# Heads of 64 dimensions issued in pairs on TensorE, and the operand tensors placed anew in memory

## What is computed

```
def dilated_attention(q, k, v, ...):          # 16 heads of 64, first attention
    s = einsum('...qd,...kd->...qk', q, k); p = softmax(mask(s)); o = p @ v
def ssd_chunked(x, dt, a, b_mat, c_mat):      # 16 heads of 64, state space
    l_mat = exp(where(causal, a_cs[t] - a_cs[s], -inf)); y = (c @ b^T * l_mat * dt) @ x
def dsa_attention(q, k, v, qi, ki, wi, topk): # 16 indexer heads of 64
    logits = einsum('bqhd,bsd->bqhs', qi, ki) * IDX_DIM ** -0.5
    score = einsum('bqh,bqhs->bqs', wi, relu(logits)); idx = top_k(score, topk)
```

## The kernel before, in words

| data | before | after |
|---|---|---|
| WH, WL ring slot 0, 1, 2, 3 | 96, 224, 352, 480 | 256, 256, 256, 256 |
| XH, XL | 160 | 320 |
| MH, ML, AH2, AL2, AH4, AL4 | 288 | 320 |
| XH minus WH, modulo 256, slot 0, 1, 2, 3 | 64, 192, 64, 192 | 64, 64, 64, 64 |
| AH2 minus WH, modulo 256, slot 0, 1, 2, 3 | 192, 64, 192, 64 | 64, 64, 64, 64 |

## Time and profile before

### The profile page before, as it was taken

The page is one execution under the profiler, slowest core; times in us unless marked ns, Lnnn a source line. Parts: engine busy times, 40 slices in busy tenths (PEclk is TensorE's granted clock), DMA queues, the critical chain, the costliest instruction groups (busy, mean ns, idle before and its releaser), DMA issues.

```text
span 2735.8 us, 52761 instructions
## 1 busy us (share of the span) xinstructions
PE 2678.4 (98%) x22440; PEld 2616.3 (96%) x22440; DVE 1788.1 (65%) x2601; ACT 1340.9 (49%) x1811; POOL 111.8 (4%) x75
## 2 busy tenths in 40 slices
PE   8999999999999999999999999999899999999996
PEld 8998889899999999999899999999899999999996
DVE  6787679675555555555677786556676656665666
ACT  5464566454344443444344684444365435543543
POOL 2000021010000000000000000000400000000003
PEclk9999999999999999999999999999899999999998
DMA  6534445455555555555454456555355555555552
GB/s 236 180 136 142 155 139 173 151 193 193 193 193 193 193 193 195 193 193 188 143 171 139 164 176 202 194 196 178 134 190 195 193 194 193 194 193 193 194 191 85
DMA packets 136603, 488.45 MB, mean 179 GB/s; under 512 B 15152, under 2 KB 17584, under 8 KB 136368
## 3 DMA queue, kind: packets, MB, share of 16 engines
q1 hardware_dynamic: 136368, 485.09, 52.2%
HBM read 482.93 MB, written 2.10 MB: 177 GB/s over the span
## 4 chain that ended last, share of the span: by engine, by line
PE 94%; DVE 4%; ACT 1%; issue 1%; DMA 0%; SPq 0%; ACTq 0%; DVEq 0%
PE ps L753 93%; PE ps L756 1%; DVE WL L1694 1%; DVE xT L1694 1%; DVE XL L1702 1%; DVE T L1694 1%; DMA cst<-in_cst 0%; ACT xT L1177 0%; ACT WH L1177 0%; DVE small L1702 0%; DVE q L1694 0%; ACT P L1177 0%; DVE small L1694 0%; DVE AL L1702 0%; DVE P L1698 0%
## 5 line engine op out<-in xcount | busy, mean ns | idle before, releaser
L1694 DVE TENSOR_TENSOR WL<-raw,WH 128x1024 fp32r<-128x1024 f32 x907 | 1122.6, 1240 | 775.6 <-ACT WH L1177 774.9
L1177 ACT ACTIVATE WH<-raw 128x1024 fp32r<-128x1024 f32 x907 | 961.1, 1060 | 1317.5 <-PE ps L753 1316.0
L753 PE MATMUL ps<-XH,WH 128*128 128x256 f32 x5024 | 1406.9, 280 | 25.0 <-issue 10.8
L753 PE MATMUL ps<-XL,WH 128*128 128x256 f32 x5024 | 1393.0, 277 | 0.0
L753 PE MATMUL ps<-XH,WL 128*128 128x256 f32 x5024 | 1392.7, 277 | 0.0
L753 PEld LDWEIGHTS ps<-XH,WH 128*128 128x128 f32 x5024 | 945.0, 188 | 33.3 <-issue 28.2
L753 PEld LDWEIGHTS ps<-XL,WH 128*128 128x128 f32 x5024 | 944.6, 188 | 2.3 <-issue 1.5
L753 PEld LDWEIGHTS ps<-XH,WL 128*128 128x128 f32 x5024 | 944.2, 188 | 0.3
L753 PE MATMUL ps<-AH,WH 128*128 128x256 f32 x1856 | 515.1, 278 | 0.6 <-DVE AL L1694 0.4
L753 PE MATMUL ps<-AL,WH 128*128 128x256 f32 x1856 | 514.2, 277 | 0.0
L753 PE MATMUL ps<-AH,WL 128*128 128x256 f32 x1856 | 514.1, 277 | 0.0
(11 more groups left out here) (227 smaller groups left out, 1645.8 us busy)
## 6 DMA issues: line engine op xcount, KB each, us to landing
raw<-in_w_up SPq DMA_DIRECT2D x304, 512.0 KB, 3.5
raw<-in_w_in SPq DMA_DIRECT2D x224, 512.0 KB, 3.5
raw<-in_w_down SPq DMA_DIRECT2D x216, 512.0 KB, 3.4
raw<-in_w_out SPq DMA_DIRECT2D x64, 512.0 KB, 3.4
raw<-in_w_gates SPq DMA_DIRECT2D x64, 512.0 KB, 3.5
raw<-in_w_ckv SPq DMA_DIRECT2D x16, 512.0 KB, 3.5
raw<-in_w_cq SPq DMA_DIRECT2D x8, 512.0 KB, 4.2
raw<-in_w_co SPq DMA_DIRECT2D x8, 512.0 KB, 3.3
```

The lines of the kernel that those rows point to most:

```text
L753: return e.matmul(out, l, r, start=start, stop=True, skip_group_check=True)
L1177: return e.activation(out, x, func, **kw)
L1694: return e.tensor_tensor(out, a, b, op)
```

## The change

Two things are changed.

**Heads in pairs.** The first attention, the indexer and the state space go through the plan in units of two heads (`heads(u)`): one chain for both, one semaphore step for both, and in `sm_qk`, `sm_av`, `ssd_y` and `ix_qk` the matmuls alternate between the two heads, that is between the halves of the array. VectorE and ScalarE steps do both heads' instructions in a row; the second multiply of `ssd_out` covers both heads in one instruction. The cross-attention and the second attention (heads of 128) keep a unit for each head. A pair holds two `P` tiles at once, and `NP` rises from 3 to 4.

**Placement.** The new tile needs 2048 bytes in each partition. `SKEW` and `skewed` are gone, with their spare elements; `rcol` and `stat` move ahead of `xT`, and `gap` puts 64 bytes ahead of `XH`. The table above shows where the operands lie then. No instruction of the weight matmuls is added or removed.

```diff
 RAW = 5
 RING = 4
-SKEW = (0, 32, 64, 96)
...
-NP = 3
+NP = 4
...
+def heads(u):
+
+
+    return (2 * u, 2 * u + 1) if u < 8 else (u + 8,)
...
+    bufs = []
+    for H in heads(u):
+        bufs += [(P.P, ("sm", H), "sm_max", "sm_tr"), (P.T, ("sm", H), "sm_copy", "sm_av"),
+                 (P.B, ("sm_qk", H), "sm_qk", "sm_exp" if cross else "sm_max"),
+                 (P.B, ("sm_tr", H), "sm_tr", "sm_copy"),
+                 (P.B, ("sm_av", H), "sm_av", "co_l" if cross else "sm_out")]
+    return P.chain(t, u, steps, *bufs)
...
-        def skewed(name, n, skip, stack):
-
-            return sb(name, [128, n * 256 + 128], F32R, stack)[:, skip:skip + n * 256].rearrange("p (a t) -> p a t", t=256)
-
         s = Signals(nc, ctx, P)
+
         cst = sb("cst", [128, CN])
         cols = sb("cols", [128, VN])
+        rcol = sb("rcol", [128, 16])
+        stat = sb("stat", [128, 24])
+        assert sum(-(-n // 8) * 8 for n in (CN, VN, 16, 24)) % 32 == 0
         xT = sb("xT", [128, 16, 256])
         raw = sb("raw", [128, RAW, GRAN])
-        WH = sb("WH", [128, RING * GRAN + 128], F32R)
-        WL = sb("WL", [128, RING * GRAN + 128], F32R)
-        XH = skewed("XH", 16, 16, ctx)
-        XL = skewed("XL", 16, 16, ctx)
+        WH = sb("WH", [128, RING * GRAN], F32R)
+        WL = sb("WL", [128, RING * GRAN], F32R)
         small = sb("small", [128, 256])
         rb = sb("rb", [128, 4, 256])
-        rcol = sb("rcol", [128, 16])
-        stat = sb("stat", [128, 24])
         Ps = [sb(f"P{i}", [128, 512]) for i in range(NP)]
         Ts = [sb(f"T{i}", [128, 512]) for i in range(NT)]
+        sb("gap", [128, 16])
+        XH = sb("XH", [128, 16, 256], F32R)
+        XL = sb("XL", [128, 16, 256], F32R)
         ps = [ctx.enter_context(nc.psum_tensor(f"ps{i}", [128, 512], F32)) for i in range(8)]
...
-                MH = skewed("MH", 8, 8, p1c)
-                ML = skewed("ML", 8, 8, p1c)
+                MH = sb("MH", [128, 8, 256], F32R, p1c)
+                ML = sb("ML", [128, 8, 256], F32R, p1c)
...
-            AH2 = skewed("AH2", 16, 8, p2)
-            AL2 = skewed("AL2", 16, 8, p2)
+            AH2 = sb("AH2", [128, 16, 256], F32R, p2)
+            AL2 = sb("AL2", [128, 16, 256], F32R, p2)
...
-            a = (g % RING) * GRAN + SKEW[g % RING]
+            a = (g % RING) * GRAN
...
-            def ssd_spread(h):
-                out, acs = S("ssd_spread", h), dts[:, 5, :]
+            def ssd_spread(u):
+                out, acs = S("ssd_spread", u), dts[:, 5, :]
                 on.wait_ge(*s("dt_acs", 1))
-                free_S(on, "ssd_spread", h)
-                spread(out[:, 0:128], acs[:, h:h + 1])
-                spread(out[:, 128:256], acs[:, 16 + h:17 + h]).then_inc(s["ssd_spread"], 1)
-
-            def ssd_y(h):
-                out, d, o = S("ssd_y", h), Pt("ssd", h), slice(64 * (h % 2), 64 * (h % 2) + 64)
-                on.wait_ge(*s("ssd_mask", h + 1))
-                on.wait_ge(*s("xs_mul", h // 4 + 1))
-                free_S(on, "ssd_y", h)
-                mm(out[o, 0:256], xsd[:, 0, h * 64:h * 64 + 64], d[:, 0:256])
-                mm(out[o, 128:256], xsd[:, 1, h * 64:h * 64 + 64], d[:, 256:384], start=False).then_inc(s["ssd_y"], 1)
+                free_S(on, "ssd_spread", u)
+                for i in range(2):
+                    for t in range(2):
+                        a, h = 256 * i + 128 * t, 2 * u + i
+                        m = spread(out[:, a:a + 128], acs[:, 16 * t + h:16 * t + h + 1])
+                m.then_inc(s["ssd_spread"], 1)
+
+            def ssd_y(u):
+                two_heads = (2 * u, 2 * u + 1)
+                on.wait_ge(*s("ssd_mask", u + 1))
+                on.wait_ge(*s("xs_mul", u // 2 + 1))
+                for h in two_heads:
+                    free_S(on, "ssd_y", h)
+                for t in range(2):
+                    for h in two_heads:
+                        out, d, o = S("ssd_y", h), Pt("ssd", h), slice(64 * (h % 2), 64 * (h % 2) + 64)
+                        m = mm(out[o, 128 * t:256], xsd[:, t, h * 64:h * 64 + 64], d[:, 256 * t:256 + 128 * t], t == 0)
+                m.then_inc(s["ssd_y"], 1)
...
+                for H in heads(u):
+                    free_S(on, "sm_qk", H)
                 for t in range(2):
-                    b = a + 128 * blocks[t]
-                    m = mm(out[:, a:b], q[:, t * 128:t * 128 + 128], k[:, 0:128 * blocks[t]])
-                    a = b
+                    for H in heads(u):
+                        out, (q, k, _, blocks), (a, b) = S("sm_qk", H), head(H), spans(H)[t]
+                        m = mm(out[:, a:b], q[:, t * 128:t * 128 + 128], k[:, 0:128 * blocks[t]])
                 m.then_inc(s["sm_qk"], 1)
...
-                a = 128 * (2 - blocks[0])
-                mm(out[:, 0:256], v(0), p[:, 0:256])
-                mm(out[:, a:256], v(1), p[:, 256:512 - a], start=False).then_inc(s["sm_av"], 1)
+                for H in heads(u):
+                    free_S(on, "sm_av", H)
+                for k in range(2):
+                    for H in heads(u):
+                        out, p, (_, _, v, blocks) = head_out(H), T("sm", H), head(H)
+                        a = 128 * (2 - blocks[0]) if k else 0
+                        m = mm(out[:, a:256], v(k), p[:, 256 * k:256 * k + 256 - a], k == 0)
+                m.then_inc(s["sm_av"], 1)
...
-            def ix_qk(h):
-                out, f, o = S("ix", h), h // 2, slice(64 * (h % 2), 64 * (h % 2) + 64)
-                on.wait_ge(*s("qi_rope", h // 4 + 1))
+            def ix_qk(u):
+                two_heads = (2 * u, 2 * u + 1)
+                on.wait_ge(*s("qi_rope", u // 2 + 1))
                 on.wait_ge(*s("kw_ki", 1))
-                free_S(on, "ix", h)
-                mm(out[:, 0:128], qi[o, f, 0:128], ki[o, 0:128])
-                mm(out[:, 128:384], qi[o, f, 128:256], ki[o, 0:256]).then_inc(s["ix_qk"], 1)
+                for h in two_heads:
+                    free_S(on, "ix", h)
+                for t in range(2):
+                    for h in two_heads:
+                        o = slice(64 * (h % 2), 64 * (h % 2) + 64)
+                        m = mm(S("ix", h)[:, 128 * t:128 + 256 * t], qi[o, u, 128 * t:128 * t + 128],
+                               ki[o, 0:128 + 128 * t])
+                m.then_inc(s["ix_qk"], 1)
...
-            def ix_relu(h):
-                free_T(on, "ix", h)
-                on.wait_ge(*s("ix_qk", h + 1))
-                fn(T("ix", h)[:, 0:384], S("ix", h)[:, 0:384], ACT.Relu, scale=0.125).then_inc(s["ix_relu"], 1)
+            def ix_relu(u):
+                on.wait_ge(*s("ix_qk", u + 1))
+                for h in (2 * u, 2 * u + 1):
+                    free_T(on, "ix", h)
+                    m = fn(T("ix", h)[:, 0:384], S("ix", h)[:, 0:384], ACT.Relu, scale=0.125)
+                m.then_inc(s["ix_relu"], 1)
...
-    for h in range(16):
-        t = P.chain(max(E("qi", 1) - 2 + h, qi + 1 if h > 11 else 0), h, ("ix_qk", "ix_relu", "ix_acc"),
-                    (T, ("ix", h), "ix_relu", "ix_acc"), (B, ("ix", h), "ix_qk", "ix_relu"))
+    for u in range(8):
+        bufs = []
+        for h in (2 * u, 2 * u + 1):
+            bufs += [(T, ("ix", h), "ix_relu", "ix_acc"), (B, ("ix", h), "ix_qk", "ix_relu")]
+        t = P.chain(max(E("qi", 1) - 2 + 2 * u, qi + 1 if u > 5 else 0), u, ("ix_qk", "ix_relu", "ix_acc"), *bufs)
```

More of the change, by code:

```diff
@@ L345, in make_plan @@
     out, sq = [], []
-    for h in range(16):
-        out.append(head_steps(P, h, rope[3] + 1 + 2 * h if h < 8 else rope[7] + 1))
+    for u in range(8):
+        out.append(head_steps(P, u, rope[3] + 1 + 4 * u if u < 4 else rope[7] + 1))
     for u in range(4):
-        t = max(out[4 * u + 3], E("v", 1)) + 1
+        t = max(out[2 * u + 1], E("v", 1)) + 1
         P.chain(t, u, ("ma_hi", "ma_lo"))
@@ L693, in head_scale, with sm_root, spans @@
             return 0.125 if H < 16 else 128.0 ** -0.5
-        def sm_root(H):
-            return root(9 + P.P.of["sm", H])
+        def sm_root(u):
+            n, x = 2 * len(heads(u)), root(9 + P.P.of["sm", heads(u)[0]])
+            return [x[:, n * i:n * i + n] for i in range(4)]
+        def spans(H):
+            a = 128 * head(H)[3][0]
+            return (0, a), (a, a + 256)
         def sync(e):
@@ L1303, in sm_copy, with sm_exp @@
-            def sm_copy(H):
-                w = 128 * sum(head(H)[3])
-                free_T(on, "sm", H)
-                on.wait_ge(*s("sm_tr", H + 1))
-                fn(T("sm", H)[:, 0:w], S("sm_tr", H)[:, 0:w], ACT.Copy).then_inc(s["sm_copy"], 1)
-            def sm_out(H):
-                on.wait_ge(*s("sm_av", H + 1))
-                to = head(H)[0]
-                if 16 <= H < 20:
+            def sm_exp(u):
+                _, bias, sums, _ = sm_root(u)
+                on.wait_ge(*s("sm_max", u + 1))
+                for i, H in enumerate(heads(u)):
+                    p = Pt("sm", H)
+                    x = S("sm_qk", H) if 16 <= H < 20 else p
```

(35 more changed lines are left out.)

221 lines of the change are left out of this document (104 added, 117 removed).

## The result

| | median us | lowest to highest | runs |
|---|---|---|---|
| before | 2735.87 | 2732.25 to 2736.43 | 4 |
| after | 2749.83 | 2748.50 to 2752.97 | 4 |

The ratio is 1.0055 (95% interval 1.0038 to 1.0073): slower, as forecast, but by 14.0 us between the medians, and by 12.4 between the two profiled spans (2735.8 and 2748.2), where the sum said 54.

The account below looks back on a forecast made before the run. TensorE, with a matmul in flight 98% of the span, was taken to bound the kernel. +79.5 − 19.5 − 6 = +54 us on 2735.8 gave 2790 us; range 2722 to 2806, the forecast's own 2774 to 2806.

Parts of the forecast that it names:

- The sign: Whole kernel: slower than before, 2790 us forecast; chance 0.79 of slower by more than 5.5 us.
- Term 1: Weight matmuls: 739 narrow granules go from 113.3 to 117.8 ns a step, plus swapped jobs; +79.5 us, bounds +70 to +82.
- The places that end the wide spacing are gone: Weight ring: with offset 64 in every slot and for every operand, no slot entry ends the 117.8 ns spacing.
- The first interruption sets it off: Weight matmuls: the first interruption, or load waits at the start, begins the 117.8 ns spacing; counted in 56 of 57 granules.
- lower bound of +70: Weight matmul spacing: least expected cost, if a few early granules stay narrow or the norms' waits take up a little.
- wide only in part: Rival, 8%: something ends the wide spacing in long stretches without interruptions; half the spacing cost, 2750 us.
- Terms 2 and 3: Interruptions: overlap of the array's halves in 30 pairs, −19.5 us, and fewer interruptions, −6 us; −25.5 us together.
- Term 4: Moved VectorE and ScalarE work: cost 0, covered by free time; TensorE's waits on heads, 3.6 us, may change by ±4 us.
- Alternating at 0: Paired heads' matmuls: halves already overlap without alternating between heads, so alternation itself is worth 0.
- The swapped jobs at 233 to 234 ns in all slots: Swapped jobs, 229 to 230 ns at offset 192 before, take 233 to 234 in every slot; +0.8 us for 16 granules.
- Offset 192 ends it: Weight ring before: a wide spacing reaching a slot of offset 192 without interruption ends, 31 of 46; at 64, 0 of 25.
- Placement is immaterial: Rival, 11%: spacing depends on something other than operand distance and its mix stays; only −25.5 us, 2710 us.

Follow-up runs that it names:

- pairs with the old ring: Changed kernel with ring slots of WH and WL shifted 0, 32, 64, 96 elements again, offsets 64, 192, 64, 192; 2699.91 us, ratio 0.9871 to before.
- uniform 192: Changed kernel with a 48-element gap ahead of XH, activations 192 bytes past the weights modulo 256 in every slot; 2741.16 us, ratio 1.0033 to before.
- ring with one step: Changed kernel with ring slots shifted 0, 32, 32, 32 elements, offsets 64, 192, 192, 192; 2700.27 us, ratio 0.9871 to before.

## Why the prediction was right and wrong

- **The sign** was right for the reason given: the placement costs more than the pairs earn. Placement alone costs 71 us (2805.69 beside 2734.51), pairs with the old ring gain 35 (2699.91 beside 2734.51).
- **Term 1, +79.5: the step that failed.** It measured +48.2 (47.5 and 0.7), and accounts for 31.3 of the 41.6 us that the sum was over. "The places that end the wide spacing are gone" holds: 0 of 498. "The first interruption sets it off" doesn't hold for every interruption, and the sum took 56 of 57 as always. With nothing left to change the spacing between interruptions, each outcome is held until the next one, so one narrow outcome counts with the length of what follows; the interruption ahead of 257 granules without another was one of the 7 in 92. It was less of an accident than 7 in 92 says, since it is of the short kind (3 of 7); the trace of before had four short ones at offset 64, all wide, so it could not have told me. The lower bound of +70 left this out. With it wide, the spacing would be 89.4, and term 1 +75.6, inside its bounds; the placement-alone kernel shows that case with 88.8.
- **The rival "wide only in part"** named the first MLP and 2750 us, with a chance of 8%. The number was hit, half by luck: nothing ended the wide spacing in the stretch, it never began there, and term 1 was 61% of its size, not half.
- **Terms 2 and 3, −25.5: mis-sized.** They measured −33.1. With three tiles pairing measures −26.7 (−24.9 without the end piece), so the overlap of the halves and the shared interruptions were right to 1.2 us. Nearly all of the rest is the fourth tile, which had no term.
- **Term 4, 0 ± 4**: right that the bursts cost nothing. The wait for `P` fell from 3.6 to 1.0 us, by the fourth tile (it lies inside interruptions, and is in their 33.1). Of the 3.4 us in the column of waits, 1.9 are the half-clock stretch behind the cross-attention; the rest is spread over waits under 2 us.
- **Alternating at 0**: right, by the kernel without it. The rule on strict order of start, from the Trainium skill (TensorE: Matmul & The Clock Gate, "Part 3: Packing small matmuls — row/col tiling"), would have taken most of term 2 away there; it gave 173.1 us of interruptions beside 172.5. The count in the earlier trace rows alone would fit strict order too, where the first six rows are also four and two; a shorter window of before, 354.44 to 354.70 us, decides. All four rows of 64x128, two of each head, have started in it, and none of 64x256:

```profile
L753 PE MATMUL ps<-kT,qT 64*128 64x128 f32 x4 | 0.5, 322 | 0.0
```

The single starts in the trace are 354.447 and 354.461, 354.661 and 354.674, and the first two of 64x256 are at 354.772 and 354.786: two heads run side by side, some 14 ns apart.

- **The swapped jobs at 233 to 234 ns in all slots**: right. Second and last matmul of granules 146 and 450, ten steps in 2.33 us each, where the earlier trace rows had 2.28 and 2.34:

```profile
499.90 0.39 PE L770 MATMUL ps<-WH,AL 128*128 128x512 f32 x1
...
502.23 0.40 PE L770 MATMUL ps<-WL,AH 128*128 128x512 f32 x1
...
1358.79 0.39 PE L770 MATMUL ps<-WH,XL 128*128 128x512 f32 x1
...
1361.12 0.39 PE L770 MATMUL ps<-WL,XH 128*128 128x512 f32 x1
```

- **"Offset 192 ends it"** was the reading of the cause, and it was half of it. The counts of before (31 of 46 at 192, none of 25 at 64) hold two things that always went together there, being at 192 and having come from 64. The uniform 192 and the ring with one step took them apart. For the forecast it made no difference; for the cure it did: I expected the uniform 192 to save 38 to 60 us, and it saved 9. The 16 exceptions of the narrow count (655 of 671) were left without a cause in the prediction; each was a step of both operands.
- **Placement is immaterial** is out: five uniform places and two rings, with the same instructions otherwise, 2700 to 2823 us. With it goes, for this kernel, what was drawn from the Trainium skill (SBUF — State Buffer, "Who interferes with whom"), that the placement changes nothing. That TensorE waits on another engine in SBUF is not shown either; only its own two operands were moved. What in the memory or the engine makes it so stays open; the runs show only the places, the steps and the spacing.

## What to carry to other kernels

Where a state is set by chance at an interruption and held until the next, don't multiply its frequency (or take it as certain): list the longest stretches between interruptions, price each as a case of its own, and count the frequency by kind of interruption. And look at the exceptions of a count before leaving them out: where are they? In a kernel that streams matmuls back to back, the place of an operand is a parameter of the schedule: take off skews and pads only after looking at start-to-start distances in the timeline, since a busy share of 98% reads the same at 113, 118 and 120 ns. When one edit holds a new buffer, pairs and a placement, price the buffer too: here it earned 5 to 9 us by itself.

## What the runs showed of the hardware that I had not expected

- The start-to-start distance of the 128x256 float32r matmuls, each with its own weight load, depends on the distance of its two operands modulo 256 bytes: 113.3 or 117.8 ns at 64 and 192, 115 to 123 at 128, 120 at 0 (0 and 128 with the activations moved alone). At 64 and 192 it is a state that is kept for hundreds of granules, set at interruptions (at 64 wide in 85 of 92, at 192 in 46 of 94) and at delays of some 20 ns, and ended by a step of the distance from 64 to 192 (13 of 21) but not from 192 to 64 (0 of 13) or without a step (0 of 18). A step of both operands by 128 bytes, at an equal distance, began the wide spacing in 16 of 16 (kernel before).
- The same program can so differ by 28 us from run to run: 2805 to 2809 and 2778 us with the placement alone.
- After waits of 2.24 and 0.75 us of TensorE, around small matmuls, the granted clock was 0.50 over the next 4.6 us, and 1.00 again behind them; with four tiles it stayed at 1.00.
